# Expert layer with its two paths in the other order, norm parameters awaited later, memory keys and queries computed transposed

## The reference

```python
def memory_cross_attention(h, mem, wq, wkv, wo):
    q = (h @ wq).reshape(b, s, MEM_HEADS, MEM_HEAD_DIM)          # 4 heads of 256
    kv = (mem @ wkv).reshape(b, m, 2, MEM_HEADS, MEM_HEAD_DIM)
    k, v = kv[:, :, 0], kv[:, :, 1]
    sc = jnp.einsum('bqhd,bkhd->bhqk', q, k).astype(jnp.float32) * (MEM_HEAD_DIM ** -0.5)
    p = jax.nn.softmax(sc, axis=-1).astype(v.dtype)
    return jnp.einsum('bhqk,bkhd->bqhd', p, v).reshape(b, s, D_MODEL) @ wo

def moe_swiglu(h, w_router, w_gu, w_down):                        # layer 1; layer 0 has one dense swiglu
    logits = (t @ w_router).astype(jnp.float32)                   # 8 experts, the best 2 for each row
    top_logit, top_idx = lax.top_k(logits, TOP_K)
    top_w = jax.nn.softmax(top_logit, axis=-1)
    gate = jnp.einsum('tk,tke->te', top_w, jax.nn.one_hot(top_idx, N_EXPERTS)).astype(h.dtype)
    for e in range(N_EXPERTS):
        out = out + gate[:, e:e + 1] * swiglu(t, w_gu[e], w_down[e])
```

## Time and profile before

| | us |
|---|---|
| median of 3 runs | 2242.58 |
| lowest and highest | 2241.51, 2242.91 |
| the profiled execution's own time | 2243.09 |
| its span (first to last instruction) | 2241.3 |
| TensorE busy | 2162.9 (97% of the span) |
| VectorE busy | 521.9 (23%) |
| ScalarE busy | 269.4 (12%) |
| GpSimd busy | 65.0 (3%) |
| HBM traffic | 485.38 MB, 217 GB/s over the span |

### The profile page before, as it was taken

How to read it: one execution, slowest core, us unless ns; L and a number is a source line. 1 busy time by engine, 2 the same in 40 slices (tenths; PEclk the granted TensorE clock), 3 DMA queues, 4 the chain that set the end, 5 groups by cost and what they waited for, 6 DMA issues and landing times.

```text
span 2241.3 us, 26934 instructions
## 1 busy us (share of the span) xinstructions
PE 2162.9 (97%) x12198; PEld 1169.0 (52%) x12198; DVE 521.9 (23%) x1068; ACT 269.4 (12%) x561; POOL 65.0 (3%) x70
## 2 busy tenths in 40 slices
PE   7999999999999999988999999999999699999998
PEld 3887445987458874543333333333333354754883
DVE  2413223001132131223010001100000389332021
ACT  1242001001013310010000000000000032420000
POOL 0000000000000000000000000000000025000000
PEclk9999999999999999998999999999999899999999
DMA  7524432433245244143999998799999542325230
GB/s 279 216 76 156 182 150 89 174 141 118 99 192 198 94 169 169 75 169 148 384 400 385 399 398 359 292 391 393 386 402 393 209 187 94 113 99 216 99 150 19
DMA packets 38422, 485.38 MB, mean 217 GB/s; under 512 B 4336, under 2 KB 4368, under 8 KB 6816
## 3 DMA queue, kind: packets, MB, share of 16 engines
q1 hardware_dynamic: 34976, 465.70, 52.1%
q0 software_dynamic: 3328, 17.90, 2.0%
HBM read 482.53 MB, written 1.05 MB: 216 GB/s over the span
## 4 chain that ended last, share of the span: by engine, by line
PE 95%; DVE 2%; DMA 2%; ACT 1%; issue 0%; DVEq 0%; SPq 0%; PEldq 0%
PE pair L331 49%; PE bank L331 46%; DMA norm_par<-in_norms 1%; DVE att L1407 0%; DMA weights<-in_even_in 0%; DMA weights<-in_w_in 0%; DVE big L1407 0%; ACT hT L2236 0%; DVE att L2012 0%; ACT big L2220 0%; DVE stats L1459 0%; DVE h L1468 0%; DVE h L1466 0%; DVE big L1994 0%; DVE h L1821 0%
## 5 line engine op out<-in xcount | busy, mean ns | idle before, releaser
L331 PE MATMUL bank<-weights,att 128*32 128x512 f32 x4224 | 457.8, 593 | 0.0
L331 PE MATMUL pair<-weights,big 128*32 128x512 f32 (+1 forms) x1968 | 395.9, 592 | 3.4 <-DVE big L1895 1.7
L331 PEld LDWEIGHTS bank<-weights,att 128*32 128x32 f32 x4224 | 135.0, 110 | 306.5 <-issue 306.3
L331 PEld LDWEIGHTS pair<-weights,big 128*32 128x32 f32 (+1 forms) x1968 | 151.7, 133 | 237.3 <-issue 232.6
L331 PE MATMUL pair<-hT,weights 128*128 128x256 f32 (+1 forms) x1344 | 254.3, 352 | 0.8 <-ACT hT L2236 0.8
L331 PE MATMUL pair<-weights,hT 128*128 128x512 f32 (+1 forms) x576 | 247.0, 589 | 3.4 <-DMA weights<-in_w_in 2.0
L331 PEld LDWEIGHTS pair<-hT,weights 128*128 128x128 f32 x1344 | 228.2, 193 | 29.7 <-issue 4.2
L331 PE MATMUL bank<-hT,weights 128*128 128x256 f32 x960 | 213.8, 382 | 0.0
L331 PEld LDWEIGHTS bank<-hT,weights 128*128 128x128 f32 x960 | 180.3, 190 | 31.5 <-issue 8.0
L331 PEld LDWEIGHTS pair<-weights,hT 128*128 128x128 f32 x576 | 109.8, 192 | 134.9 <-issue 130.9
L1801 DVE TENSOR_TENSOR big<-head_gain,bank 128x256 f32<-128x256 f32 x66 | 27.8, 421 | 424.0 <-ACT head_gain L2347 424.0
(11 more groups left out here) (272 smaller groups left out, 1310.4 us busy)
## 6 DMA issues: line engine op xcount, KB each, us to landing
weights<-in_moe_up SPq DMA_DIRECT2D x88, 2048.0 KB, 10.4
weights<-in_moe_down SPq DMA_DIRECT2D x40, 2048.0 KB, 10.8
weights<-in_w_in SPq DMA_DIRECT2D x18, 2048.0 KB, 7.5
weights<-in_ffn_up SPq DMA_DIRECT2D x11, 2048.0 KB, 7.2
weights<-in_even_in SPq DMA_DIRECT2D x10, 2048.0 KB, 8.4
weights<-in_mem_wkv SPq DMA_DIRECT2D x8, 2048.0 KB, 7.1
weights<-in_odd_in SPq DMA_DIRECT2D x8, 2048.0 KB, 7.2
norm_par<-in_norms POOLq DMA_DIRECT2D x10, 1024.0 KB, 11.1
```

The source lines that it names most:

```text
L331: ins = pe.matmul(o, lhsT, rhs, **flags)
```

## The change

In the expert layer the general path is placed first on PE, DVE, ACT and SP (`If(largest > FEW)`), the few-row path second, so that its last instruction is followed in the program by the common code. DVE's `ffn(1)` no longer waits for the second set of norm parameters ahead of `moe`, but in `row(0)`, right before `pre_row`. In the memory stage K and Q come from `product_T` in transposed form and are copied straight to `hv`; the 32 transposes of K and Q go, and the natural K and Q buffers with them. The first half of V stays a product in natural order, and the order of the weight tiles stays as it was.

```diff
@@ PE, cross @@
-                product(("kv", l), memT_at, KD, [512] * 3, KD)
+                for c in range(2):
+                    product_T(("kT", l, c), lambda kk: memT[:, kk, :], KD)
+                product(("v0", l), memT_at, KD, [512], KD)
                 pe.wait_ge(*L.next("normed", 2))
                 transpose_rows(("hT", "mem", l), lambda t, kk: h[:, t, kk * P:(kk + 1) * P], KD)
-                transpose_rows(("xkT", l), lambda t, kk: k[:, t, kk * P:(kk + 1) * P], KD)
                 pe.wait_ge(*emptied((("hT", "mem", l), KD - 2)))
-                product(("q", l), hT_at, KD, [512] * 2, KD)
-                pe.wait_ge(*emptied((("q", l), 1)))
-                transpose_rows(("xqT", l), lambda t, kk: q[:, t, kk * P:(kk + 1) * P], KD)
-                pe.wait_ge(*emptied((("xqT", l), KD - 2)))
+                for c in range(2):
+                    product_T(("qT", l, c), lambda kk: hT[:, kk, :], KD)
+                pe.wait_ge(*emptied(("qT", l, 1)))
@@ PE, moe @@
-                with pe.If(largest < FEW + 1):
-                    few_gather(0)
...
-                with pe.Else():
+                with pe.If(largest > FEW):
                     for s in range(NSLOT):
                         pe.wait_ge(*L.at(f"slot{s}_landed", 16 * (rounds[s] + 1)))
...
+                with pe.Else():
+                    few_gather(0)
+                    few_group(0)
+                    few_gather(1)
+                    few_sum(0)
+                    few_group(1)
+                    few_sum(1)
...
@@ DVE, cross @@
-                for c in range(3):
-                    dst = k if c < 2 else memory
-                    copy((("kv", l), c), dst[:, :, 512 * (c % 2):512 * (c % 2) + 512])
+                for c in range(2):
+                    copy(("kT", l, c), hv[:, 8 + 4 * c:12 + 4 * c, :].rearrange("p (a b) t -> p a (b t)", a=2))
+                copy((("v0", l), 0), memory[:, :, 0:512])
                 copies(("hT", "mem", l), hT, KD)
-                copies(("xkT", l), hv[:, 8:16, :], KD)
                 for c in range(2):
-                    copy((("q", l), c), q[:, :, 512 * c:512 * c + 512])
-                copies(("xqT", l), hv[:, 0:8, :], KD)
+                    copy(("qT", l, c), hv[:, 4 * c:4 * c + 4, :].rearrange("p (a b) t -> p a (b t)", a=2))
@@ DVE, moe @@
-                with ve.If(largest < FEW + 1):
+                with ve.If(largest > FEW):
+                    gates()
+                    with L.loop(N_EXPERTS, PER_EXPERT) as ex:
+                        ffn_body(("ffn", 1), bass.ds(ex, 1))
...
+                L.seen = start
+                with ve.Else():
                     picks(0)
                     gates()
                     gated_picks(0)
...
@@ DVE, ffn @@
-                    after, g = norm_slot(), norm_slot()[0]
+                    after = norm_slot()
                     def row(t):
                         row_stats(h, t)
                         row_norm(t, *after)
-                        pre_row(t, g)
+                        if t == 0:
+                            ve.wait_ge(*L.next("norm_par1_landed", 16))
+                        pre_row(t, norm_par[:, 1, 0, :])
                     moe(row)
                     row(1)
-                    ve.wait_ge(*L.at("normed", L.seen["normed"]))
+                    norms[0] += 1
+                    rows_normed()
@@ ACT and SP: the same exchange of If and Else @@
-                        with act.If(largest < FEW + 1):
+                        with act.If(largest > FEW):
+                            with L.loop(N_EXPERTS, PER_EXPERT):
+                                ffn_body(("ffn", l))
+                        with act.Else():
                             for g in range(N_GROUPS):
```

More of the change, by code:

```diff
@@ L1072, in moe @@
                 largest = pe.value_load(most_i[0:1, 0:1], min_val=0, max_val=T)
-                start = (counts(), list(pairs.uses), list(banks.uses), tiles_used[0], dict(L.seen))
+                start = (counts(), tuple(pairs.uses), tuple(banks.uses), tiles_used[0], dict(L.seen))
                 def begun():
@@ L1851, in moe @@
                             ve.sem_inc(sems(name), to_come(name, n))
[L1852 to L1869 removed]
+                    for name, n in FEW_STEPS.items():
+                        assert L.seen[name] == n
             def ffn_body(name, col):
@@ L2617, in _ @@
                         largest = sp.value_load(most_i[0:1, 0:1], min_val=0, max_val=T)
-                        with sp.If(largest < FEW + 1):
-                            for tile in order[NSLOT:]:
-                                into(*tile)
                         n[0] = first + NSLOT
-                        with sp.Else():
+                        with sp.If(largest > FEW):
                             before = n[0]
@@ L2628, in _ @@
                         assert n[0] == first + NSLOT * EACH_ROUNDS
+                        with sp.Else():
+                            for tile in order[NSLOT:]:
+                                into(*tile)
                         n[0] = first + NSLOT * ALL_ROUNDS
```

74 lines of the change are left out of this document (29 added, 45 removed).

## The result

| | median, us | fastest to slowest | profiled span, us |
|---|---|---|---|
| before (4 runs in this comparison) | 2242.74 | 2241.51 to 2243.67 | 2241.3 |
| after (4 runs) | 2226.42 | 2226.08 to 2226.90 | 2225.0 |

The ratio is 0.9928, with an interval of 0.9913 to 0.9943: a gain of 16.3 us, where 17.9 were forecast; the forecast of 2224.7 is 1.7 us too low, and the range held the time.

What follows compares the result with a forecast made beforehand. The prediction took TensorE, busy 97% of the span, as the bound. From 2243.09 it took 9.36 (norm), 7.2 (memory stage) and 2.29 (hole), added 1.0 (entry): 2225.2, or 2224.7 us as median; 8-in-10 range 2221.0 to 2230.0.

Steps and rivals of the forecast that it cites:

- the hole: Even block's start, after 7 of 8 transposes: PE's stall for code behind the jump goes, gaining 2.29 us.
- the entry: Start of the expert layer's paths: the jump over the general path, now here, costs 1.0 us in all.
- The norm wait: Entry of layer 1's expert layer: DVE no longer waits for norm parameters, so routing starts 9.36 us earlier.
- The memory stage: K and Q without transposes: scores start 3.59 us earlier in a layer, 7.2 us for both.
- lower bound of 2.5 us: Memory stage, both layers: the gain left if transposed products cost 0.5 us each more than the odd block shows.
- rival 1: Exit: tiles crowding the DMA engines cause the hole whatever the code's order, so it stays; 2227.0 us, chance 0.13.
- 0.8 us over: Entry on PE: a fetch priced at 2.5 us, less 1.7 us of cover while the gather waits for picks.
- Adding 0.3 for DVE: Entry on DVE: the jump over the general path's body delays the first pick by 0.3 us.
- Rival 2: Entry cold and dear on DVE and PE: 4 to 7 us instead of 1; 2229.2 us, chance 0.14.
- rival 3: Gather: shorter stillness keeps the clock up or raises it sooner, 1.7 us more gain; 2223.0 us, chance 0.07.
- the chain of 8.54 us: Exit: from issue to landing of the even block's first weight tile, 8.54 us, taken to stay unchanged.
- Rival 4: Expert stream becomes bound by the DMA engines, each of 34 steps waits; 2252 us, slower than before, chance 0.03.

Runs made afterwards that it cites:

- e2: The kernel before with only the memory-stage edits (K and Q transposed, both layers): median 2233.38 us.
- e4: The kernel after with the few-row path first again on PE alone: median 2227.41 us.
- e9: The kernel before with 16 idle matmuls at PE's start, shifting all of PE's later code: median 2238.08 us.
- e12: A second run of e4, the kernel after with the few-row path first on PE alone: median 2225.61 us.
- e1: The kernel before with only DVE's wait for the second norm parameters moved to row(0): median 2233.41 us.
- e5: The kernel after with the general path's loop left out on PE, so the entry jump has a near target: median 2224.72 us.
- e6: The kernel after with slots 0 and 1 counted up before the last sums, so SP issues the even block's tiles earlier: median 2218.35 us.
- e8: The kernel after with 40 idle matmuls on PE in the three waits before the branch: median 2227.82 us.
- e10: e6 with the picks and group 0's gather moved ahead of reading the count and the branch, for both paths: median 2216.55 us.
- e3: The kernel before with only the two paths exchanged on PE, DVE, ACT and SP: median 2242.01 us.
- e11: The kernel after, unchanged, run a second time: median 2226.35 us.
- e7: e6 with the few-row path first again on PE: median 2224.98 us.

## Why the prediction was right, and where it wasn't

The two large terms of the sum came nearly whole. Of the two small ones the hole was right in size for an incomplete reason, and the entry was put at half of what it cost; three terms of 0.7 to 1.6 us weren't in the sum at all.

**The norm wait: 9.36 forecast, 8.95 measured.** The mechanism is as read: the router product replaced the transfer as the last to come. The 0.4 us are the wake-up of DVE, 995.52 to 995.96, for which 0.04 had been taken; in the earlier trace rows DVE had been busy until then, so no row there showed what a waiting DVE needs. The wait itself varies by more, 10.2 to 11.9 us in the four profiles that have it: with the 10.23 of e2, 9.36 would have been 7.7.

**The memory stage: 7.2 forecast, 6.7 measured.** Q's products took 27.89 us where the earlier trace rows gave 27.71, and Q began 0.1 later than worked out. A price from another stage was good to 1%. The lower bound of 2.5 us doesn't follow from the forecast's own numbers, 3.59 less 2 for a layer, which give 3.2 for both; the sum didn't use it.

**The hole at the exit: 2.29 forecast, 2.41 measured, and the reason incomplete.** The forecast read it as the second piece behind the jump, and the packet at 1782.03 bears that out. But it took jump and tiles to be enough, and rival 1 the tiles alone. Neither is: e2, e4, e9 and e12 have jump and tiles and no hole. It takes a place of the code at which PE needs the second piece before it is there. Edits that shift PE's code have this gain by themselves: e2, e4 and e9 did, and e1, which leaves PE's code alone, keeps 1.71 us of the hole. So it is partly luck that the term was right: by e4 the change would have had the 2.41 us with PE's order as it was. The forecast's remark that the code that runs on is fetched ahead fits the after trace (1737.26, then nothing until 1780.61).

**The entry: 1.0 forecast, 2.18 measured.** 0.13 of it on DVE, for which 0.3 had been taken, and 2.05 on PE. The step that failed is "0.8 us over": a small fetch was priced by the landing of a data tile of 256 KB, 2.5 us, and 1.7 us of cover were taken off. The packet began at 1002.69 and took 1.57, and from its end to the gather at 1005.80 another 1.54 went by: 3.11 us and not 2.5. Of these only the 1.03 until the picks were ready at 1003.72 were covered, not 1.7. 3.11 - 1.03 is the 2.08 of the chain. Adding 0.3 for DVE was a slip beside it: the gather starts with the later of picks and code, and the forecast's own 1017.8 + 2.5 is 0.85 after 1019.45, whatever DVE does. Rival 2 priced this at 4 to 7 and had DVE in it; its mechanism was half right, since the target was cold and dear on PE alone. By the Trainium skill (Runtime: NRT & Kernel Launch, Instruction fetch mechanics) a taken branch to a target outside the pages held forces a fetch. The traces agree: e5 differs by the distance of the target, and has no stall, and no packet until 1008.99.

**Not in the sum at all:** -1.63 in the gather, by the clock. The forecast left this cost "as it is", and rival 3 had the sign reversed: the clock came up 6.2 us after the gather's start and not 2.8. Over the fourteen profiles it took 12.6 to 14.5 us from the gather's start to the first group, in no order that follows the edits (before 12.63, e6 12.72, e8 12.90, e5 13.73, e10 14.54). What sets the moment stays open. Two profiles of the kernel after agree (14.26 and 14.05), two of the one with PE's order back less so (13.97 and 13.42), and e6, whose code at the entry is that of the kernel after, had 12.72.

+1.24 at the tile's landing. The forecast said that the chain of 8.54 us "is the transfer and stays". It didn't stay: it is 7.31 after. In every profile in which the tile is in the chain and a code packet of 16 KB falls into the landing of that tile it takes 8.2 to 8.7 us (before, e1, e2, e3, e4, e8, e9, e12), and where none does, 7.2 to 7.3 (after, e5, e11): 11 of 11 (in e6, e7 and e10 it isn't in the chain). No run set this alone, so it is a correlation; that the packet delays the tile is not shown. It doesn't follow the order of the paths either: e3 and e8 run on without a jump, have a packet in the landing, and took 8.6. So at the exit the kernel after gained 1.2 + 2.4, where 2.29 had been counted, and both hang on where its code lies. The +0.66 behind them is the clock in the `u` product, 9.22 us and not 9.86.

Rival 4 didn't occur: the steps of the expert stream take 20.74 us as in the earlier trace rows, and the ledger has 0.00 between the first group and the last sums. In later runs it did in a small way: PE waited for a `moe_down` tile 0.4 us in e4 and e8 and 1.2 in e7, and that row lost 0.6 to 1.5.

In all: -0.41 and -0.5 in the large terms, -1.2 and -1.6 at the entry, +0.1, +1.2 and +0.7 at the exit and +0.2 at the start give -1.5 us of the span; the forecast missed the median by 1.7. That the result lies so near is partly luck: the misses add up to 3.7 us one way and 2.2 the other.

## What to carry to other kernels

Give a jump a price at its target: some 2 us on TensorE for a cold one with idle DMA engines, several if weight tiles are in flight, nothing for a near one; and put it where a transfer or other work covers it. Whether tiles issued behind the fetch rather than ahead of it would leave it cheap was not tried. A hole of "issue" with all semaphores satisfied behind a jump can go away with an edit that only shifts code, so test a shift of the code alone before crediting an edit with it. Separate gains may contain the same hole, so look row by row in the ledgers before adding medians. And repeat a profile before a term of 1 to 2 us is credited to an edit: the clock in the first product and in the gather, and the wait for the norm parameters, moved by as much with no edit that touched them.

## What the runs showed of the hardware

- Code comes to TensorE in packets of 16 KB, which take 0.9 to 1.6 us; where PE stood for one, its next instruction started 1.3 to 1.7 us after the packet's end (before 1782.99 to 1784.36, after 1004.26 to 1005.80, e1 1772.50 to 1773.84, e7 1763.65 to 1765.39).
- Behind a jump that falls together with the issue of five 2 MB tiles the first packet began 3.9 to 4.3 us after the first issue (six kernels); with the DMA engines idle 0.6 us after DVE's first pick (after).
- A stall for code can come at the second packet behind a jump: 2.3 us that 16 matmuls at the kernel's start took away.
- With a code packet in its landing a 2 MB tile took 8.2 to 8.7 us, without one 7.2 to 7.3 (a correlation, 8 profiles against 3).
- With weight tiles in flight a jump stood 6.67 us (e7), the same kind of jump with idle DMA engines 2.08 (after), and one to a near target 0.06 (e5).
- Matmuls of no use keep the granted clock up for small work that follows (the router product 1.95 us, not 3.58) and bring it up earlier at the kernel's start (first product 14.21 us, against 15.48 to 17.07 in thirteen profiles without them). In the gather the clock fell all the same: 0.54 over 3 us.
